# A hybrid decoder layer: compression products among transposes, an earlier turn for the sample tokens, and a last norm by halves

## The reference, cut to what matters

```
proj = x @ w_in        # q, k/v of two mixers, window k/v, branch gates, two merge gates
o_a  = nsa_attention   # compressed blocks (k and v summed over 32 tokens with weights),
                       # top-16 selected blocks, a sliding window; sigmoid gates
o_b  = moba_attention  # blocks of 256, top-3 past blocks and the own one
m    = sigmoid(gA) * (o_a @ w_branch_a) + sigmoid(gB) * (o_b @ w_branch_b)
h    = LN(alpha * x + m @ w_out) * g1 + b1
s    = (h @ wq) . keys             # 8 heads, two halves of 128 keys each
e, g = top 16 of the 256 sums of the two top-16 lists, softmax of their scores
f    = sum over heads and k of g * gelu(h . u[e]) * v[e]
y    = LN(alpha * h + f) * g2 + b2
```

## Time and profile before

| | us |
|---|---|
| time, median of 3 runs (1122.59 to 1131.11) | 1128.77 |
| the profiled execution's own time | 1126.86 |
| its span, first to last instruction | 1125.2 |

### The profile page before, as it was taken

The page is one execution under the profiler, slowest core; times in us unless marked ns, Lnnn a source line. Parts: engine busy times, 40 slices in busy tenths (PEclk is TensorE's granted clock), DMA queues, the critical chain, the costliest instruction groups (busy, mean ns, idle before and its releaser), DMA issues.

```text
span 1125.2 us, 14422 instructions
## 1 busy us (share of the span) xinstructions
PE 960.7 (85%) x3923; PEld 546.2 (49%) x3923; DVE 630.1 (56%) x1610; ACT 348.7 (31%) x1081; POOL 360.2 (32%) x417
## 2 busy tenths in 40 slices
PE   7998889999999998899899999687587777787774
PEld 6885466666667884446455553233133233233320
DVE  0002146572112587785774856896867766866446
ACT  1223133321000123444243343243234234243221
POOL 3320120011200025443344334444244443444440
PEclk9999989999999999999999999999888998899998
DMA  9875398886977579999999999999989999999994
GB/s 352 278 266 192 118 344 245 239 299 258 348 296 282 187 291 396 420 401 420 376 416 372 406 375 376 413 410 392 414 332 394 415 422 387 423 420 421 420 422 171
DMA packets 77064, 388.34 MB, mean 345 GB/s; under 512 B 11337, under 2 KB 14481, under 8 KB 42633
## 3 DMA queue, kind: packets, MB, share of 16 engines
q0 software_dynamic: 44000, 300.21, 66.4%
q1 hardware_dynamic: 28928, 82.68, 21.1%
q10 hardware_dynamic: 4080, 4.78, 1.2%
HBM read 384.55 MB, written 7.27 MB: 348 GB/s over the span
## 4 chain that ended last, share of the span: by engine, by line
PE 47%; DVE 20%; DMA 18%; issue 9%; ACT 4%; POOL 1%; SPq 0%; DVEq 0%; POOLq 0%; ACTq 0%
DMA big<-peer_uv,idx_r 16%; PE ps L1262 15%; PE ps L850 8%; DVE big L1755 7%; PE ps L1032 4%; PE ps L1146 3%; PE ps L891 3%; DMA big<-wall 1%; POOL big L572 1%; PE ps L1219 1%; PE ps L981 1%; PE ps L1087 1%; PE ps L1131 1%; PE ps L983 1%; PE ps L928 1%
## 5 line engine op out<-in xcount | busy, mean ns | idle before, releaser
L1262 PE MATMUL ps<-big,kv_n 128*128 128x512 f32 x1024 | 492.6, 630 | 117.9 <-ACT kv_n L762 115.8
L572 POOL DMA_INDIRECT big<-peer_uv,idx_r x264 | 289.1, 1095 | 399.9 <-PE ps L1262 330.3
L1755 DVE CUSTOM_DVE_ANT_0 big<-big,x_n 128x1024 f32<-128x1024 f32 x256 | 307.8, 1225 | 153.0 <-DMA big<-peer_uv,idx_r 140.8
L1262 PEld LDWEIGHTS ps<-big,kv_n 128*128 128x128 f32 x1024 | 196.7, 200 | 385.6 <-issue 212.1
L752 ACT ACTIVATE gel<-dots 128x2 f32<-128x2 f32 x132 | 26.9, 203 | 361.1 <-DVE dots L1755 360.2
L762 ACT ACTIVATE kv_n<-cst,wts 128x128 f32<-128x128 f32 (+1 forms) x264 | 90.8, 391 | 4.3
L850 PE MATMUL ps<-xT_r,ring 128*128 128x264 f32 x368 | 84.7, 395 | 7.4 <-DMA ring<-wall 7.4
L850 PEld LDWEIGHTS ps<-xT_r,ring 128*128 128x128 f32 x368 | 71.6, 195 | 20.2 <-issue 7.4
L758 ACT ACTIVATE wts<-gk,gel 128x1 f32<-128x1 f32 (+1 forms) x256 | 61.4, 287 | 12.8 <-ACT gel L752 0.3
L1146 PEld LDWEIGHTS ps<-xT_r,ring 128*128 128x128 f32 x512 | 61.2, 191 | 7.4 <-issue 7.4
L1146 PE MATMUL ps<-xT_r,ring 128*128 128x128 f32 (+1 forms) x512 | 64.4, 280 | 0.0
(11 more groups left out here) (318 smaller groups left out, 962.9 us busy)
## 6 DMA issues: line engine op xcount, KB each, us to landing
ring<-wall SPq DMA_DIRECT2D x65, 512.0 KB, 6.1
ring<-pack_kv SPq DMA_DIRECT2D x80, 320.0 KB, 3.4
big<-pack_cmp POOLq DMA_DIRECT2D x42, 128.0 KB, 3.6
ring<-pack_kv POOLq DMA_DIRECT2D x16, 320.0 KB, 5.7
pg_r<-pack_kv SPq DMA_DIRECT2D x16, 320.0 KB, 7.8
pg_r<-pack_kv POOLq DMA_DIRECT2D x16, 320.0 KB, 6.7
big<-peer_uv,idx_r POOLq DMA_INDIRECT x264
big<-wall SPq DMA_DIRECT2D x2, 2048.0 KB, 13.9
```

The lines of the kernel that those rows point to most:

```text
L572: pool.indirect_dma_start(uv_rows[:, slot, :], None, a["peer_uv"], off).then_inc(uv_in[slot], 16)
L1262: last = mm(ps[:, 4 + 2 * tt + c, :], diag[:, q, s, :], row, start=False, stop=stop)
L1755: v.tensor_tensor_reduce(out=uv_rows[:, slot, 0:D], in0=uv_rows[:, slot, 0:D], in1=hrow, scale=1.0, scalar=0.0, op0=ALU.mult, op1=ALU.add, ...
```

## The change

It has three parts, each with some edits around it.

1. The compression's products start behind the first two groups of transposes; the other ten groups and the two gate transposes stand between the first six product groups of weight 0. The sigmoid of the gates moves behind ScalarE's first group copy. Merge gate 0 stands behind the products, gate 1 behind the first scores; both read the first copy of the inputs, so GpSimd waits for gate 1 before it clears it. Gates 2, 3 and 4 stand under the softmax chain, gate 5 ahead of the values, the other ten behind them; the gates' slots are shifted by one, and `MRG_AHEAD` is 6.
2. The sample's turn stands behind head 1 of tile 1 on all engines, and its norm behind head 2; `deviation` and the waits follow.
3. The last norm takes two passes, ((x - mean) * g) * rstd + b: the first over all columns, ahead of the wait for the root, the second in two halves, each written out by its own DMA. The last rows of tile 1 are added by halves, and the first half's statistics wait for the first half alone.

The diff, cut to its core:

```diff
+SAMPLE_TURN = P // 8 + 2 * HEAD_T
...
-        slot = n % RING if n < W_MRG else (n - W_MRG) % PGRING if n < W_BRANCH else ...
+        slot = n % RING if n < W_MRG else (n - W_MRG + 1) % PGRING if n < W_BRANCH else ...
...
-        vc_dT = xT_r[:, 0:NB * NCMP_D]
+        vc_dT = big[:, 4608:4608 + NB * NCMP_D]
...
-        MRG_AHEAD = 4
-        MRG_BANK = [(3, 4, 3)[i] if i < 3 else i % 2 for i in range(16)]
+        MRG_EARLY = 2
+        MRG_AHEAD = 6
+        MRG_BANK = [(3, 6, 3, 4, 3)[i] if i < 5 else i % 2 for i in range(16)]
         EXP_AFTER = (0, 0, 1, 1)
-        MRG_BEHIND = [(4,), (5, 6), (7,), (8, 9), (10,), (11, 12), (13,), (14, 15)]
+        MRG_BEHIND = [(6,), (7,), (8, 9), (10,), (11,), (12, 13), (14,), (15,)]
...                                                                # SP's queue
-            for n in range(turns * RING, W_MRG):
+            for n in range(turns * RING, W_MRG + MRG_EARLY):
                 weight(n)
...
                     load_chunk(0, 1, 0, 1, None)
-                    for n in range(W_MRG, W_MRG + PGRING):
-                        weight(n)
+                    weight(W_MRG + MRG_EARLY)
...
+            for n, (out, rows) in enumerate(...):                  # tile 0, sample, tile 1
+                for c in range(2):
+                    sp.wait_ge(y_sb, 2 * n + c + 1)
+                    sp.dma_start(out[:, c * 512:(c + 1) * 512], rows[:, c * 512:(c + 1) * 512]).then_inc(out_y, 16)
...                                                                # GpSimd
+            pool.wait_ge(w_used, W_MRG + MRG_EARLY)
             own(pool.memset(xT_r[:, :], 0.0))
...
             for tt in range(2):
                 rows_of_head(tt, 0)
-                with pool.Fori(1, NH) as h:
+                if tt == 1:
+                    rows_of_head(tt, 1)
+                    pool.wait_ge(eis_in, 16 * NH)
+                    fetch_turn(SAMPLE_TURN, 2, eidx_s[:, :])
+                with pool.Fori(1 + tt, NH) as h:
                     rows_of_head(tt, h)
...                                                                # ScalarE
+            merge_copy(0)
             exps(0, 0)
+            merge_copy(1)
...
-            done = 0
+            done = MRG_EARLY
             for i, v in enumerate((pc, pm, psl, pw)):
                 for _ in range(EXP_AFTER[i]):
                     merge_copy(done)
                     done += 1
                 act.wait_ge(dmax_sb, i + 1)
...                                                                # TensorE
+            rows_of_keys(0)
+            rows_of_keys(1)
...
+                    if c == 0 and i == 0:
+                        pe.wait_ge(kcx_sb, 8)
                     last = mm(ps[:, 1 + c, 0:36]..., w, kcx..., start=(i == 0), stop=(i == 7))
+                    if c == 0 and i < 5:
+                        rows_of_keys(2 * i + 2)
+                        rows_of_keys(2 * i + 3)
+                    if c == 0 and i == 5:
+                        pe.wait_ge(gates_sb, 1)
+                        for tt in range(2):
+                            gate = tp(...)
...
+            pe.wait_ge(kvt_a, 6)
+            merge_gate(0)
             pe.wait_ge(comp_sb, 6)
...
             scores(0, 0, 0)
+            merge_gate(1)
             pe.wait_ge(vct_sb, 1)
+            pe.wait_ge(proj_sb, T_MRG + 2 + 1)
...
-            merge_gate(0)
+            merge_gate(2)
             pe.wait_ge(dmax_sb, 1)
-            merge_gate(1)
-            merge_gate(2)
+            merge_gate(3)
+            merge_gate(4)
             pe.wait_ge(pd_sb, 1)
...
-            merge_gate(3)
-            pe.wait_ge(proj_sb, T_MRG + 2 + 3)
+            merge_gate(5)
+            pe.wait_ge(proj_sb, T_MRG + 2 + 5)
...
+            def add_last_rows():
+                pe.wait_ge(diag_sb, SLOTS * TURNS)
+                at = kept(1, 7, GROUPS - 1)
+                for s in range(UNROLL):
+                    last = add_row(1, diag[:, at, s, :], SLOTS - UNROLL + s, 0, s == UNROLL - 1)
+                last.then_inc(sum0_mm, 1)
+                for s in range(UNROLL):
+                    add_row(1, diag[:, at, s, :], SLOTS - UNROLL + s, 1, s == UNROLL - 1).then_inc(v_used, 1)
...                                                                # VectorE
+            def layer_norm(tt, src, summed):
+                for c in range(2):
+                    dve.wait_ge(*summed[c])
+                    own.loose(v.bn_stats(stats[0:r, 6 * c:6 * c + 6], src[:, c * 512:(c + 1) * 512]))
...
+                own.loose(STT(xr, src, stats[0:r, 12:13], ln_rows[0:r, 2, :], ALU.subtract, ALU.mult))
                 dve.wait_ge(std_sb, norms[0] + 1)
                 own(v.reciprocal(stats[0:r, 14:15], stats[0:r, 15:16]))
-                own(TS(xr, src, stats[0:r, 12:13], stats[0:r, 14:15], ALU.subtract, ALU.mult))
-                own(TT(xr, xr, ln_rows[0:r, g, :], ALU.mult))
-                TT(xr, xr, ln_rows[0:r, g + 1, :], ALU.add).then_inc(done, 1)
+                for c in range(2):
+                    half = slice(c * 512, (c + 1) * 512)
+                    STT(xr[:, half], xr[:, half], stats[0:r, 14:15], ln_rows[0:r, 3, half], ALU.mult, ALU.add).then_inc(y_sb, 1)
...
             tile_out(0)
-            heads(1, 1, 6, per)
+            steady(1, 1)
+            for q in range(TURN_G):
+                dot(TURN_G * SAMPLE_TURN + q, q, SAMPLE_TURN, h_rep)
+            steady(1, 2)
+            tile_out(2)
+            heads(1, 3, 6, per)
             head(1, 6, {0: [(1, 7, 2)], 1: [(1, 7, 3)]}, {6: [(1, 7, 2 * NH + 1)]})
             head(1, 7, {}, {})
-            for q in range(TURN_G):
-                dot(TURN_G * TURN0[2] + q, q, TURN0[2], h_rep)
             tile_out(1)
-            tile_out(2)
```

More of the change, by code:

```diff
@@ L772, in head_group @@
                     act.wait_ge(nm_sb, found(tt, h))
-                weights(h * GROUPS + (TURN_G * TURN0[tt] + q), q,
+                weights(h * GROUPS + (TURN_G * turn0(tt, h) + q), kept(tt, h, q),
                         lambda s: gk[:, tt, bass.ds(h * TOPK + (q * UNROLL + s), 1)])
@@ L828, in _ @@
             deviation(0)
-            heads(1, 1, 7)
+            for q in range(GROUPS):
+                head_group(1, 1, q)
+            act.wait_ge(gks_in, 16 * NH)
+            for q in range(TURN_G):
+                weights(TURN_G * SAMPLE_TURN + q, q, lambda s: gk_s[:, q * UNROLL + s:q * UNROLL + s + 1], sample=True)
+            for q in range(GROUPS):
+                head_group(1, 2, q)
+            deviation(2)
+            heads(1, 3, 7)
             for q in range(GROUPS):
                 head_group(1, 7, q)
-            act.wait_ge(gks_in, 16 * NH)
-            for q in range(TURN_G):
-                weights(TURN_G * TURN0[2] + q, q, lambda s: gk_s[:, q * UNROLL + s:q * UNROLL + s + 1], sample=True)
             deviation(1)
-            deviation(2)
         @block.tensor
@@ L859, in _, with rows_of_keys @@
             pe.wait_ge(cst_in, 16)
-            for g in range(12):
+            def rows_of_keys(g):
                 if g >= 2:
@@ L871, in _ @@
                 last.then_inc(kvt_mm, 1)
-            pe.wait_ge(gates_sb, 1)
-            for tt in range(2):
-                last = tp(ps[:, 0, tt * P:(tt + 1) * P], feat[:, T_GATE, tt * P:(tt + 1) * P], ident)
-            last.then_inc(kvt_mm, 1)
+            rows_of_keys(0)
+            rows_of_keys(1)
             pe.wait_ge(ct_in, 16 * (NB * NPG - 2 * (T_MRG // 2)))
             pe.wait_ge(cta_in, 16 * 2 * (T_MRG // 2))
-            pe.wait_ge(kcx_sb, 8)
             pe.wait_ge(pe_in, 16)
@@ L1021, in _ @@
             last.then_inc(win_mm, 1)
-            def merge_gate(i):
-                n = W_MRG + i
-                pe.wait_ge(w_in[W_SLOT[n]], 16 * W_LOADS[n])
-                if i == 0:
-                    pe.wait_ge(xT_in, 32)
-                if i >= 2:
-                    pe.wait_ge(proj_sb, T_MRG + 2 + (i - 1))
-                for k in range(KD):
-                    last = mm(ps[:, MRG_BANK[i], 0:T], ring[:, W_SLOT[n], k * P:(k + 1) * P], xT2[:, k, :], start=(k == 0), stop=(k == KD - 1))
-                last.then_inc(w_used, 1)
             pe.wait_ge(oT_v, 1)
@@ L1250, in residual, with add_row @@
                         mm(ps[0:NB, c, :], alpha_id[0:NB, 0:NB], x_n[0:NB, 2, c * 512:(c + 1) * 512], start=True, stop=False)
+            def add_row(tt, at, slot, c, stop):
+                row = uv_rows[:, slot, D + c * 512:D + (c + 1) * 512]
+                if tt < 2:
+                    return mm(ps[:, 4 + 2 * tt + c, :], at, row, start=False, stop=stop)
+                return mm(ps[0:NB, c, :], at, row, start=False, stop=stop)
             def add_rows(tt, h, q):
@@ L1301, in _ @@
             residual(2)
-            for tt, lo in ((0, ITEM_HEADS), (1, 0)):
-                with pe.Fori(lo, 7) as h:
-                    for q in range(GROUPS):
-                        add_rows(tt, h, q)
+            with pe.Fori(ITEM_HEADS, 7) as h:
```

(16 more changed lines are left out.)

98 lines of the change are left out of this document (55 added, 43 removed).

## The result

| | before | after |
|---|---|---|
| time, median of the runs of the comparison, us | 1129.64 | 1120.25 |
| ratio after to before, 95% interval | | 0.9923 [0.9899, 0.9948] |
| profiled execution's own time, us | 1126.86 | 1120.42 |
| its span, us | 1125.2 | 1118.4 |

The change makes the kernel 0.8% faster: by the ratio 8.7 us, by the two profiled executions 6.4, since the profile of before happens to be a short execution. The 1119 forecast lies 1.3 from the median.

The account below looks back on a forecast made before the run. Gathers bound the kernel from about 420 us; ahead of them TensorE and its waits. Terms -6.0 + 0 + 1.6 - 1.3 - 0.8 - 3.0 = -9.5 gave 1119 us on the median's scale; 8-in-10 range 1111 to 1126.

Parts of the forecast that it names:

- Products among transposes: Compression stage: transposes of keys between product groups no longer wait for copies; 36.1 us instead of 42.1, so -6.0.
- Two gates behind: Gate 0 behind the products, gate 1 behind the first scores, in TensorE's idle time: net 0, bounds -1.2 to +1.7.
- Wait for gate 3's weights: Under the softmax chain: weight 3 queues behind value pages, TensorE idles some ten us, values start later: +8.9.
- Rival 3: TensorE's lower clock after gate 3's wait lasts through gates 3 to 5 and the transposes: 1131 to 1133 us; chance 0.06.
- Two gates fewer among the values: Values stage: two merge gates fewer run there, -7.3 us.
- Branch weights: Ahead of the output weights: 0.5 MB less loads behind the last gate, -1.3 us, bounds 0 and -2.5.
- Tile 0's norm: Among the gathers: two passes by halves shorten the norm, so 2.6 us of the DMA engines' idle go: -2.6.
- The sample's norm: Newly among the gathers: costs 4.6 us of VectorE and so what is left of the DMA idle: +1.8.
- The end: From the last dot to the end: 11.5 to 12.2 us instead of 15.2; -3.0 taken.
- Rival 1: Gate 3's weights are in time, so the 8.9 us wait goes: 1110 us; chance 0.09.

Follow-up runs that it names:

- the kernel with the old norm: The kernel after, with the last norm as before: whole rows, three passes, whole outputs, last products unsplit; 1129.15 us, ratio 1.0002 to before.
- the kernel with early weights: The kernel after, with weights of gates 3 and 4 loaded right behind the last key pages; 1114.91 us (0.9858 of before), run again 1112.32 (0.9841).
- half-way: The kernel after, with weights of gates 3 and 4 behind the first four of the queue's eight value pages; a single execution, 1117.22 us.

## Why the prediction was right

The total was right, and most of its steps; one term was mis-sized, and the wait's price was short by the clock of one gate.

- **Products among transposes, -6.0:** measured -6.3, in after and in the run of the part alone (42.1 to 35.8 from the first transpose to the end of the products). Right. What the prediction did not say is that the six does not pass on by itself: alone, 3.8 to 4.3 reach the first dot. In the two stretches that lose the two us TensorE works at a lower clock (0.60 instead of 0.72 behind the products, and 5.4 us for the same transposes instead of 4.5); that holding up the clock would bring them to the first dot is not shown.
- **Two gates behind, net 0:** the first decode scores are 6.0 earlier in after, 0.8 of it from ahead of the transposes, so this step is +1.1, within its bound of 1.7. Three other profiles with the same stage at a clock of 1.00 had those scores 8.1 earlier. GpSimd was done at 144.8, 2.3 ahead of the scores: covered.
- **Wait for gate 3's weights, +8.9:** measured +10.6 (values +5.0 against gate 2's -5.6). The mechanism was right, and three runs show it. The weight came 0.5 later than forecast, counted from the queue's start; the other 1.2 is mostly the clock: one gate was priced at the lower level and one at the upper (9.0 together), and the pair took 10.36, at 0.70, since the clock stood at 0.50 from gate 3's start to 256 and at 0.56 to 257. The price had been taken from a gate that followed short transposes, where the lower level was over in 3.2; behind ten us of idle it lasted some 6. Rival 3 so came true for the better part of the two gates, and not beyond: 1.00 in the transposes behind. The Trainium skill's rule on a ring's order (DMA: Bandwidth & Descriptors, section Queues, rings and completion order) gave 256.0 on before's scale, and weight 3 landed at 250.7 + 5.6 = 256.3: the trace agrees to 0.3.
- **Two gates fewer among the values, -7.3:** -7.1. **Branch weights, -1.3:** -1.9, within its bound, but good to about a us only: the kernel with the old norm, which shares this code, has -1.1 (16.36 from the first branch product to the output product, 15.58 in after, 17.45 in before).
- **Tile 0's norm, -2.6:** dots 136 to 160 took 69.7 to 71.3 in five profiles with the old norm, 66.0 to 68.7 in seven with the new in one block, means 70.2 and 67.0: -3.2. Right, and the hole that is left, 2.6, is near the two that were forecast.
- **The sample's norm, +1.8:** mis-sized. Its hole alone is 3.3, since the finds of the next head stand behind it as behind tile 0's, and the means above put the whole turn at 4.5. "What is left of the idle" was taken from a hole that another norm had already shortened; a norm at a new place opens the whole of its own.
- **The end, -3.0:** -3.45 (16.33 to 12.88). The output's second half, 256 KB, was done 2.45 behind its issue (1115.95 to 1118.4), near the 32 KB's 2.24. The Trainium skill's fit (DMA: Bandwidth & Descriptors, section Anatomy of one DMA — SWDGE (gpsimd) path) is stated for GpSimd's DMAs, and this output goes by SP's queue; carried over, it gave an estimated 2.6, and the trace agrees to 0.15.

In medians the forecast was -9.5 and the measurement -9.4. The two profiled spans differ by 6.8 only: by their landmarks the wait was 1.7 dearer than forecast, the stage between the products and gate 2 1.5, the gathers 1.4, and the other steps together 2 better. That the medians agree to 0.1 is therefore luck in part: errors of 4.6 one way and 2 the other, and the spread of the gathers. The ratio's interval, -5.9 to -11.4 us, holds both figures. Against the forecast's picture stands what the parts show: the products and the shorter norms make the whole gain, the early gates are worth nothing as their weights are loaded, and the sample's move costs more than it saves: with the short norms it opens a hole of 3.3 us and the end is no shorter (12.9 with the turn earlier, 12.4 with it last), with the old norm it opens one of 6.0 and the end is 0.9 shorter (15.4, and 16.3). Rival 1's place was right too: with the weights in time the kernel takes 1112 to 1115, where it said 1110.

Open: why identical code between dot 164 and dot 263 takes 245.4 in one profile and 252.0 in another, and how much of the sample's 4.5 is more than its hole.

## What to carry to other kernels

When work is moved to an earlier place, its successor in line moves up too, and what that successor needs was loaded for the old time: follow the queue that loads it before counting the gain. In a stage that transfers bound, a block on an engine of the chain that frees the buffers can leave the DMA engines empty: here a norm 2.4 us longer made holes 2.4 and 2.7 longer, and the same work in two pieces, where that engine has no other block, made none. A gain ahead of a stage with idle time can shrink in it: here six us became four, with TensorE's clock at 0.60 instead of 0.72 behind the gain, so look there and not only inside it, and compare the same work, not the same window of time.

## What was not expected of the hardware

From the products' end to the first decode scores TensorE was granted 0.72 of the upper level twice with the old order, 0.58 and 0.60 with the products earlier and no gates, and 0.84 to 1.00 in nine profiles with gates in its idle time; where it was 1.00 the scores came 17.4 us behind the products' end, gates included, at 0.58 and 0.60 after 19.95 without them. The same program, the kernel with early weights, got 0.86 in one profile and 1.00 in another. The gate behind the transposes of probabilities took 5.3 to 6.8 us instead of 3.83 in eleven profiles in which TensorE had waited 1.3 for VectorE ahead of the transposes; directly behind gates 3 and 4 it took 3.83 in two (after, and the old norm) and 5.51 in one (half-way).
